# One-hot product of a gate token as two 128-column matmuls accumulated in PSUM, in place of one of 256 columns and a VectorE addition

## The reference, cut to what matters

```
eid  = top 16 of (i1 * 128 + i2)              # 8 heads x 16 picks = 128 picks per token
gate = softmax(top_s)
act  = gelu(einsum('chkd,cd->chk', u_emb[eid], x))
out  = einsum('chk,chkd->cd', gate * act, v_emb[eid])
```

## Time and profile before

| what | value |
|---|---|
| time, median of three executions | 1237.27 us (1237.13 to 1238.29) |
| span of the profiled execution, first to last instruction | 1236.2 us |
| median less that span | 1.1 us |
| granted TensorE clock, mean over the span | 0.993 of full speed |
| PE (matmul) busy | 1200.4 us, 97% |
| PEld (weight load) busy | 1114.8 us, 90% |
| DVE (VectorE) busy | 920.6 us, 74% |
| ACT (ScalarE) busy | 596.2 us, 48% |
| POOL (GpSimd) busy | 617.2 us, 50% |

### The profile page before, as it was taken

How to read it: one execution, slowest core, us unless ns; L and a number is a source line. 1 busy time by engine, 2 the same in 40 slices (tenths; PEclk the granted TensorE clock), 3 DMA queues, 4 the chain that set the end, 5 groups by cost and what they waited for, 6 DMA issues and landing times.

```text
span 1236.2 us, 28223 instructions
## 1 busy us (share of the span) xinstructions
PE 1200.4 (97%) x8839; PEld 1114.8 (90%) x8839; DVE 920.6 (74%) x2251; ACT 596.2 (48%) x1021; POOL 617.2 (50%) x313
## 2 busy tenths in 40 slices
PE   5999999989999999999999999999999999999997
PEld 3888888879989999999999999999888888888886
DVE  3899967957647999779999997000667888888865
ACT  2342546666444445445555454444555555555553
POOL 0475665603755577766666666777203444443101
PEclk9999999999999999999999999999999999999999
DMA  9786674424643466665555555667877898888773
GB/s 356 247 294 211 221 254 176 159 69 164 243 149 125 138 216 199 211 193 182 178 187 179 181 184 180 216 208 241 278 240 271 314 341 307 305 300 308 270 238 105
DMA packets 115996, 273.12 MB, mean 221 GB/s; under 512 B 32033, under 2 KB 56321, under 8 KB 115553
## 3 DMA queue, kind: packets, MB, share of 16 engines
q1 hardware_dynamic: 107760, 248.96, 59.5%
q0 software_dynamic: 6448, 19.71, 4.5%
q10 hardware_dynamic: 1728, 3.68, 0.9%
HBM read 249.30 MB, written 23.00 MB: 220 GB/s over the span
## 4 chain that ended last, share of the span: by engine, by line
PE 90%; issue 2%; DVE 2%; DMA 2%; POOL 2%; ACT 1%; SPq 1%; DVEq 0%; POOLq 0%; ACTq 0%
PE ps L2305 19%; PE ps L2247 11%; PE ps L2254 11%; PE ps L2248 11%; PE ps L2308 10%; PE ps L1909 7%; PE ps L1925 7%; PE ps L1919 6%; PE ps L2283 2%; DMA ring<-in_stream 2%; POOL split L683 1%; PE ps L1941 1%; PE ps L2013 1%; PE ps L1863 1%; PE ps L2224 1%
## 5 line engine op out<-in xcount | busy, mean ns | idle before, releaser
L750 POOL TENSOR_TENSOR split<-ring,split 128x1024 fp32r<-128x1024 f32 x128 | 307.4, 2402 | 138.7 <-ACT split L1051 138.7
L1051 ACT ACTIVATE split<-ring 128x1024 fp32r<-128x1024 f32 x256 | 271.6, 1061 | 173.5 <-PE ps L2305 168.4
L683 POOL TENSOR_TENSOR split<-ring,split 128x1024 fp32r<-128x1024 f32 x77 | 187.9, 2442 | 210.7 <-ACT split L862 204.1
L2247 PE MATMUL ps<-h2r,split 128*128 128x288 f32 x1024 | 278.6, 297 | 0.7 <-ACT big L1077 0.5
L2248 PE MATMUL ps<-h2r,split 128*128 128x288 f32 x1024 | 278.8, 296 | 0.0
L2305 PE MATMUL ps<-h2r,split 128*128 128x512 f32 x1016 | 255.3, 392 | 0.0
L2305 PEld LDWEIGHTS ps<-h2r,split 128*128 128x128 f32 x1016 | 182.8, 189 | 32.7
L2247 PEld LDWEIGHTS ps<-h2r,split 128*128 128x128 f32 x1024 | 192.9, 188 | 1.2 <-ACT big L1077 0.8
L2248 PEld LDWEIGHTS ps<-h2r,split 128*128 128x128 f32 x1024 | 192.4, 188 | 0.0
L1758 DVE TENSOR_TENSOR split<-ring,split 128x1024 fp32r<-128x1024 f32 x128 | 156.0, 1219 | 1.8 <-PE ps L2254 1.8
L1107 ACT ACTIVATE act<-ps 128x288 f32<-128x288 f32 x124 | 51.2, 413 | 219.0 <-PE ps L2254 215.9
(11 more groups left out here) (301 smaller groups left out, 1624.4 us busy)
## 6 DMA issues: line engine op xcount, KB each, us to landing
ring<-in_stream SPq DMA_DIRECT2D x371, 512.0 KB, 3.5
act_dram<-act SPq DMA_DIRECT2D x128, 128.0 KB, 1.7
big<-in_stream SPq DMA_DIRECT2D x20, 512.0 KB, 7.7
parts<-act_dram SPq DMA_DIRECT2D x16, 512.0 KB, 4.7
big<-act_dram SPq DMA_DIRECT2D x16, 512.0 KB, 5.4
big<-in_cache_k SPq DMA_DIRECT2D x16, 128.0 KB, 2.5
big<-in_cache_v SPq DMA_DIRECT2D x16, 128.0 KB, 3.4
s_act_dram<-act SPq DMA_DIRECT2D x128, 16.0 KB, 1.5
```

The source lines that it names most:

```text
L683: nc.gpsimd.tensor_tensor(split[:, n % 2, 1], ring[:, POS[CUT[n]] % R, :], split[:, n % 2, 0].bitcast(f32), ALU.subtract).then_inc(lin_lo, 1)
L750: nc.gpsimd.tensor_tensor(split[:, (n + ODD) % 2, 1], ring[:, slot_of(n), :], split[:, (n + ODD) % 2, 0].bitcast(f32), ALU.subtract).then_ ...
L1051: nc.scalar.activation(split[:, (n + ODD) % 2, 0], ring[:, slot_of(n), :], ACT.Copy).then_inc(hi_ready, 1)
L2247: MM(out, u_hi[:, k], h_hi[:, k], start=(k == 0), stop=False)
```

## The change

A token's product is made by two matmuls of 128 columns on the same stationary matrix hot2, the high half of hot1 first and the low half second, the second accumulated onto the first in PSUM (`start` on the first, `stop` on the second). A pair of tokens then fills 256 columns of its bank. ScalarE copies the finished sums and counts `gate_copied` itself. VectorE's additions, the semaphore `gate_high` and VectorE's wait for it are gone, and the last two `hot_used` waits with them.

```diff
@@ ScalarE, turn @@
-                            both = ps[2 + 2 * (n % 2) + pair][:, :].rearrange("p (t a i) -> p a i t", t=2, a=2)
+                            both = ps[2 + 2 * (n % 2) + pair][:, 0:2 * P].rearrange("p (t i) -> p i t", t=2)
                             nc.scalar.activation(gate_mat[:, :, bass.ds(g * (4 * R) + (4 * (n - BEFORE) + 2 * pair), 2)],
-                                                 both[:, 0], ACT.Copy).then_inc(gate_high, 1)
+                                                 both, ACT.Copy).then_inc(gate_copied, 1)
@@ VectorE @@
-            def gate_sum(g, pair, odd):
-
-                both = ps[2 + 2 * odd + pair][:, :].rearrange("p (t a i) -> p a i t", t=2, a=2)
-                gates = gate_mat[:, :, bass.ds(g * 4 + 2 * pair, 2)]
-                dve.wait_ge(gate_high, g * 2 + (pair + 1))
-                V.tensor_tensor(gates, both[:, 1], gates, ALU.add).then_inc(gate_copied, 1)
...
                     for j in range(2):
                         last = one_hot(g * 4 + (2 * pair + j), 2 * pair + j)
                     last.then_inc(hot_ready, 1)
-                    if not first:
-                        gate_sum(g - 1, pair, 1 - odd)
...
-            for pair in range(2):
-                dve.wait_ge(hot_used, 2 * (MIXED - 1) + pair + 1)
-                gate_sum(MIXED - 1, pair, 1)
@@ TensorE, gate_tokens @@
                 for j in range(2):
                     s = 2 * pair + j
-                    last = MM(ps[2 + 2 * (n % 2) + pair][:, j * 2 * P:(j + 1) * 2 * P], hot2[:, s],
-                              hot1[:, s].rearrange("p a i -> p (a i)"), start=True, stop=True)
+                    for part in range(2):
+                        last = MM(ps[2 + 2 * (n % 2) + pair][:, j * P:(j + 1) * P], hot2[:, s], hot1[:, s, part],
+                                  start=(part == 0), stop=(part == 1))
                 last.then_inc(hot_used, 1)
```

More of the change, by code:

```diff
@@ L552, in build @@
         gate_cut = sem("gate_cut")
-        gate_high = sem("gate_high")
         gelued = sem("gelued")
@@ L1713, in one_hot, with token_pairs @@
                                               ALU.is_equal, ALU.mult)
-            def gate_sum(g, pair, odd):
-                both = ps[2 + 2 * odd + pair][:, :].rearrange("p (t a i) -> p a i t", t=2, a=2)
-                gates = gate_mat[:, :, bass.ds(g * 4 + 2 * pair, 2)]
-                dve.wait_ge(gate_high, g * 2 + (pair + 1))
-                V.tensor_tensor(gates, both[:, 1], gates, ALU.add).then_inc(gate_copied, 1)
-            def token_pairs(g, odd, first=False):
+            def token_pairs(g, first=False):
                 for pair in range(2):
@@ L1729, in token_pairs @@
                     last.then_inc(hot_ready, 1)
-                    if not first:
-                        gate_sum(g - 1, pair, 1 - odd)
-            token_pairs(0, 0, True)
-            token_pairs(1, 1)
+            token_pairs(0, True)
+            token_pairs(1)
             with dve.Fori(1, MIXED // 2) as g:
                 for odd in range(2):
-                    token_pairs(g * 2 + odd, odd)
-            for pair in range(2):
-                dve.wait_ge(hot_used, 2 * (MIXED - 1) + pair + 1)
-                gate_sum(MIXED - 1, pair, 1)
+                    token_pairs(g * 2 + odd)
             dve.wait_ge(gate_copied, 2 * MIXED)
```

## The result

The kernel after takes 1262.14 us (median of four executions, 1260.59 to 1262.61), the kernel before, measured beside it, 1237.20 us (1234.95 to 1238.29). The ratio is 1.0203, with a 95% interval of 1.0188 to 1.0219: 24.9 us slower, where 27.3 were forecast. The profiled execution spans 1260.3 us.

What follows compares the result with a forecast made beforehand. TensorE's instruction stream was taken to bound the gate-building stretch. Profiled span 1236.2 us, plus 1.1 us to the median, plus 27.3 us for added matmuls, with removal and moved count at 0, gave 1264.6 us; range 1261.5 to 1323 us.

Steps and rivals of the forecast that it cites:

- The bound: While gates are built, 532 to 769 us, TensorE's instruction stream sets the time; additions to it reach the end in full.
- The removal costed at nothing: VectorE's 128 additions, 58.1 us, lie beside TensorE's stream, so removing them gives 0, at most 1.0 us.
- The moved count: Counting `gate_copied` at ScalarE's copy instead of VectorE's addition frees banks sooner; TensorE did not wait for them: 0.
- The added matmuls: In each mixed block, eight 128-column matmuls at 112 ns replace four of 256: +426 ns a block, +27.3 us.
- the forecast case's own bounds: Total time of the kernel after between 1262.5 and 1268.0 us, given a chance of 0.58.
- Plain fp32: Rival: narrow fp32r token matmuls run as plain fp32, two 112 ns pieces each; +84.6 us, 1321.9 us, chance 0.18.
- Second load hidden: Rival: a token's second load of the same hot2 weights is hidden; +14.7 us, 1252.0 us, chance 0.07.
- No load exposed: Rival: the queue hides fp32r loads even behind 63 ns of columns; +2.2 us, 1239.5 us, chance 0.05.
- The loop's code: Rival: the longer loop body makes TensorE fetch code again each iteration, adding 18 to 54 us; chance 0.09.
- What I named as the sign: Profile after: two tokens' matmuls as 0.45 us chain pieces, mixed blocks 4.11 us apart, VectorE's share about 60%.

Runs made afterwards that it cites:

- the kernel before with one group: Kernel before with both token pairs' four 256-column matmuls placed together behind the block's low matmuls: 1237.43 us beside 1236.05 us, ratio 1.0011.
- the width experiment: Kernel after with each token's two matmuls at 32, 192 or 256 columns in place of 128: 1260.60, 1263.87 and 1266.68 us.
- one bf16 group: Kernel after with hot1 and hot2 in bf16 and all eight 128-column matmuls of a block in one group: 1239.88 us, ratio 1.0022 to before.
- the bf16 one with 256 columns: Kernel before with hot1 and hot2 in bf16, one 256-column matmul a token, additions kept: 1237.29 us, ratio 1.0001 to before.
- the first bf16 one: Kernel after with hot1 and hot2 in bf16, two 128-column matmuls a token in two groups: 1241.01 us, ratio 1.0033 to before.
- the spread kernel: Kernel after with a block's eight narrow matmuls placed one by one among those of 288 columns: 1261.46 us beside 1236.87 us, ratio 1.0191.

## Why the prediction was right

**The bound.** That TensorE's stream alone sets the time of the stretch held in every kernel but one: time followed the stream's length and nothing else. The one is the kernel before with one group, where the loop's branch, behind a late count of VectorE's, took 55 ns a block.

**The removal costed at nothing** was right, and exactly: 3.687 us a block with the additions and without. The cover is PE's stream, and VectorE's wait for `hot_used` took the place of the additions. I had expected its share at about 60%; it is 68%. I had taken the additions' 58.1 us off the 216 us as a whole. But the three groups of the earlier trace rows sum to 269.5 us where VectorE was busy for 216, so its instructions overlap, and without the additions (169.67 us in the same window) only 46 us were gone.

**The moved count** cost nothing: no wait of PE for `gate_copied` or `hot_ready` appeared in the kernel after.

**The added matmuls.** This is the step that carried the forecast, and its term was slightly too large. I took 112 ns from matmuls of 32 columns in another part of the kernel; hot2's took 111. Those were loads of plain fp32, and no row showed that loads of fp32r weights cost the same; that was assumed from their shown lengths, 188 ns beside 187 to 192, and it held. Eight of them are 888 ns, where I had 896, and with the wide matmuls a block grew by 414 ns where I had 426: 26.5 us and not 27.3. My sentence that a stream of loads and matmuls doesn't go below some 110 ns was too wide: with two-byte weights it is 56 ns. (By columns it should read 63.2 ns, not 63.1, which changes nothing.) The total of 1262.14 us lies 0.4 us under the forecast case's own bounds, which is less than executions of one kernel differ by, and within the range given. The far end of the range was for the fall to plain fp32, which the width experiment excludes.

**The rivals.** Plain fp32: out, by one record a matmul and 111 ns at 32, 128 and 192 columns. Second load hidden: out, since other weights change nothing, and since 60 ns is only the first distance in a group. No load exposed: out, by 4.100 us a block. The Trainium skill's figure of about 81 ns for such a stream ("TensorE: Matmul & The Clock Gate", "Back-to-back issue gap") fits neither type here: 111 ns with four-byte and 56 ns with two-byte weights. The loop's code: out, by 34 pieces with a body of 256 and 35 with one of 320 loads and matmuls, and by none that comes in between the loop's first iteration and its end. The two-page window that the Trainium skill, "Runtime: NRT & Kernel Launch", section "Instruction fetch mechanics", describes didn't show itself on TensorE, though a body of this size may still lie within two pages, so no run here tests it. The Trainium skill gives TensorE, in the same section, four times the instruction memory of most engines; nothing in these traces speaks against that.

**What I named as the sign** was wrong in one more place: pieces of 0.45 us for a pair. They are 0.40, and the missing 0.05 us stands in the next line of the chain. By the token matmuls' own pieces the change would cost 0.79 - 0.47 = 0.32 us a block, where in truth it costs 0.414; only the block's period shows the whole.

## What to carry to other kernels

On a path bound by TensorE, count weight loads as well as columns: with four-byte weights a matmul costs 111 ns at 32, 128 and 192 columns alike (up to about 240, an estimate from 0.434 ns a column), so splitting one of 256 columns in two nearly doubles its price. Accumulating in PSUM saved another engine's addition, and that was worth nothing where the engine was beside the path; where it is on the path the sum may come out otherwise, which no run here shows. Spreading narrow matmuls among wide ones or repeating the same weights doesn't help; wider matmuls or two-byte weights do, and then the four-byte load behind a narrow matmul still needs something to hide beside. Judge such a change by the period of the loop, not by the matmuls' own entries, since a late load is charged to the next line. And look at the wait in front of a loop's branch: with its count 0.4 us later, the last experiment lost 55 ns a block there.

## What the runs showed besides

- **A load leads by one matmul, and it shows behind the group.** 60, 110, 111, 112 ns and then 51 ns late at the second wide matmul; with 32 columns 28 ns first and 87 ns late; the sum for each matmul is 111 and 112 ns.
- **The matmuls of 288 columns don't always take the same time.** From start to start they take 133.9 ns in the mixed blocks of the kernels before, after, without additions, with 192 columns and with one bf16 group, and 134.7 ns in the bf16 one with 256 columns, but 131.4 to 132.3 ns in those with 32 or 256 columns, the first bf16 one and the kernel before with one group; the spread kernel's 132.8 ns lie between. Over 24 matmuls and 64 blocks that is 2.5 to 3.8 us, more than some of the terms above, and it moved against or with three of my expectations. In the kernel before the slowest of them (145 and 152 ns) stand about 0.5 us behind the start of ScalarE's rounding of the next tile, and so they do without the additions, in the kernel after and with 192 columns; with 32 columns the matmuls there take 135 ns or less. Whose traffic it is stays open; no run here took ScalarE's part away.
